# Moving the eight Toeplitz copies of a decoder layer's bias from ScalarE's queue to SyncE's

## The reference, cut to what matters

```
def step(S, xs):
    q_i, k_i, vw_i, kcd_i, qk_i, g_i = xs
    v_new = vw_i - jnp.einsum('bhck,bhkv->bhcv', kcd_i, S)
    o_i = ... + jnp.einsum('bhij,bhjv->bhiv', qk_i, v_new)
    S = S * jnp.exp(g_end)[..., None, None] + jnp.einsum('bhck,bhcv->bhkv', ..., v_new)
```

## Time and profile before

| what | us |
|---|---|
| median of 3 runs | 3125.3 (3123.02 to 3129.53) |
| the profiled execution, its own time | 3125.3 |
| its span, first to last instruction | 3123.6 |
| `delta_rule` in the profile, about | 775 to 1127 |

### The profile page before, as it was taken

How to read it: one execution, slowest core, us unless ns; L and a number is a source line. 1 busy time by engine, 2 the same in 40 slices (tenths; PEclk the granted TensorE clock), 3 DMA queues, 4 the chain that set the end, 5 groups by cost and what they waited for, 6 DMA issues and landing times. The chain is left out here.

```text
span 3123.6 us, 53938 instructions
## 1 busy us (share of the span) xinstructions
PE 2768.1 (89%) x22092; PEld 2499.9 (80%) x22092; DVE 1328.7 (43%) x2374; ACT 861.2 (28%) x1595; POOL 666.5 (21%) x499
## 2 busy tenths in 40 slices
PE   8999999998777859997559999877899999999996
PEld 7999999998566735554229999864699999999996
DVE  5999986130333456663123453031223332323224
ACT  4333112131222337772123122041222112121222
POOL 1222212111333200001224334100042122212223
PEclk9999999999788889996559999998699999999998
DMA  4112252322655430004654441214111111111111
GB/s 168 55 50 93 88 106 83 96 72 92 200 159 164 133 129 30 30 1 155 222 166 166 143 161 41 90 67 190 54 48 42 48 48 48 41 48 48 41 48 63
DMA packets 152232, 290.91 MB, mean 93 GB/s; under 512 B 29163, under 2 KB 97708, under 8 KB 149589
## 3 DMA queue, kind: packets, MB, share of 16 engines
q1 hardware_dynamic: 128278, 242.93, 24.1%
q0 software_dynamic: 9984, 27.28, 2.9%
q10 hardware_dynamic: 13728, 17.31, 1.6%
HBM read 246.50 MB, written 51.93 MB: 96 GB/s over the span
## 5 line engine op out<-in xcount | busy, mean ns | idle before, releaser
L152 POOL TENSOR_TENSOR mlp_w_low<-mlp_w_raw,mlp_w_high 128x1024 fp32r<-128x1024 f32 x72 | 173.7, 2412 | 853.5 <-ACT mlp_w_high L148 853.5
L336 PE MATMUL in_psum<-x_high,in_w_high 128*128 128x352 f32 x1416 | 266.8, 330 | 24.2 <-DVE x_low L531 14.3
L152 POOL TENSOR_TENSOR in_w_low<-in_w_raw,in_w_high 128x1024 fp32r<-128x1024 f32 x59 | 145.2, 2462 | 575.6 <-ACT in_w_high L148 575.6
L2728 PE MATMUL mlp_psum<-mlp_in,mlp_w_high 128*128 128x352 f32 x1536 | 264.9, 324 | 0.0
L336 PEld LDWEIGHTS in_psum<-x_high,in_w_high 128*128 128x128 f32 x1416 | 236.7, 191 | 32.8 <-issue 17.5
L336 PE MATMUL in_psum<-x_low,in_w_high 128*128 128x352 f32 x1416 | 259.8, 325 | 0.0
L336 PE MATMUL in_psum<-x_high,in_w_low 128*128 128x352 f32 x1416 | 258.6, 324 | 0.0
L2728 PEld LDWEIGHTS mlp_psum<-mlp_in,mlp_w_high 128*128 128x128 f32 x1536 | 251.2, 189 | 0.2
L148 ACT ACTIVATE mlp_w_high<-mlp_w_raw 128x1024 fp32r<-128x1024 f32 x72 | 76.4, 1061 | 622.1 <-PE mlp_psum L2728 617.8
L336 PEld LDWEIGHTS in_psum<-x_low,in_w_high 128*128 128x128 f32 x1416 | 235.8, 190 | 0.0
L336 PEld LDWEIGHTS in_psum<-x_high,in_w_low 128*128 128x128 f32 x1416 | 234.3, 189 | 0.0
(11 more groups left out here) (462 smaller groups left out, 4601.4 us busy)
## 6 DMA issues: line engine op xcount, KB each, us to landing
mlp_w_raw<-in_w_mlp SPq DMA_DIRECT2D x64, 512.0 KB, 3.4
in_w_raw<-in_w_in SPq DMA_DIRECT2D x59, 512.0 KB, 4.2
u_scratch<-stage SPq DMA_DIRECT2D x32, 528.0 KB, 5.2
gdnp_page_ring<-in_cache_cmp POOLq DMA_DIRECT2D x128, 128.0 KB, 3.4
gdnp_page_ring<-in_cache_cmp SPq DMA_DIRECT2D x128, 128.0 KB, 3.3
aux<-u_scratch SPq DMA_DIRECT2D x24, 528.0 KB, 4.1
ss_ring<-in_cache_slc SPq DMA_DIRECT2D x96, 128.0 KB, 3.9
ss_ring<-in_cache_slc ACTq DMA_DIRECT2D x80, 128.0 KB, 4.0
```

Source lines behind the costliest of these rows:

```text
L152: self.nc.gpsimd.tensor_tensor(self.low[:, i % 2, 0:k * P], self.raw[:, i % 2, 0:k * P], self.high[:, i % 2, 0:k * P].bitcast(F32), ALU.su ...
L336: return mm(psum[:, e % 2, n, 0:WN], w[:, i % 2, c * P:(c + 1) * P], a[:, c, n * WN:(n + 1) * WN], start=x == 0 and c == 0, stop=x == 2 an ...
L2728: return mm(psum[:, e % 2, n, 0:WN], w[:, i % 2, c * P:(c + 1) * P], a(c)[:, column(n)], start=x == 0 and c == 0, stop=x == 2 and c == CHU ...
```

## The change

The two DMAs of `spread_bias(i)` are no longer issued by ScalarE in rounds 0, 2, 4 and 6 but by SP in rounds 0, 1, 2 and 3. In SP's loop they stand after `load(t + 2)` and ahead of the page loads of the round. The copies themselves, their sizes, their access patterns and their semaphore are the same.

```diff
@@ delta_rule, block.sync
             for t in range(NT):
                 if t + 2 < NT:
                     load(t + 2)
+                if t < NSA_HEADS // 2:
+                    rows, toeplitz = spread
+                    for off, m, to in ((0, TP, 0), (LB_FULL, 640, TP)):
+                        src = bass.AP(rows.tensor, 2 * t * (LB_FULL + LB_WIN) + off + P - 1, [[LB_FULL + LB_WIN, 2], [-1, P], [1, m]])
+                        sp.dma_start(toeplitz[2 * t:2 * t + 2, :, to:to + m], src).then_inc(rows_spread, 16)
                 for step in range(t * STEPS + RING, min((t + 1) * STEPS + RING, NB * STEPS)):
                     load_pages(sp, step, (0, 1), pages_in)
                 if t + 1 < NT:
@@ delta_rule, block.scalar
-            def spread_bias(i):
-                rows, toeplitz = spread
-                for off, m, to in ((0, TP, 0), (LB_FULL, 640, TP)):
-                    src = bass.AP(rows.tensor, 2 * i * (LB_FULL + LB_WIN) + off + P - 1, [[LB_FULL + LB_WIN, 2], [-1, P], [1, m]])
-                    act.dma_start(toeplitz[2 * i:2 * i + 2, :, to:to + m], src).then_inc(rows_spread, 16)
-
@@
             for t in range(NT):
                 behind = t >= 1
-                if t % 2 == 0:
-                    spread_bias(t // 2)
                 row_decay(t + 1)
                 keep_y(t, 1)
```

## The result

The changed kernel takes 3160.8 us (median of 4 runs, 3158.7 to 3166.2) against 3124.2 us before: a ratio of 1.0117, 95% interval 1.0099 to 1.0137. The profiled execution took 3165.1 us, so its rows show 39.6 us more span where the medians differ by 37. Every time in this document is of executions in the faster of two states of the chip; one execution of the kernel with half of the rows, at 5840.7 us, is left out.

The account below looks back on a forecast made before the run. TensorE, busy 2768.1 of 3123.6 us, was taken as the bound. Copies ahead of SP's pages delay round 7 by 88.0 us, ScalarE's 29 us gain included: 3123.6 + 88.0 + 1.7 = 3213 us; range 3165 to 3255 us.

Parts of the forecast that it names:

- The rival in which pages pass the copies inside one queue: In SP's queue, pages are served while copies are pending; only ScalarE's 29 us are left, 3096 us; chance 0.12.
- I take 44: A pair of copies in SP's queue holds its two DMA engines for 44 us, bounds 37.8 to 51.
- lag: In SP's queue, the copies' rows begin to move 5 us after issue, bounds 3 and 7.
- landing: The first SP page behind a pair lands 2 us after the pair, at most 3.
- R: Moment of `compress(t, 4)` in a round, after its wait for SP's page; 848 us in round 0, then every 66.2 us.
- my lower end: For the pair, 37.8 us at 45 GB/s; for the whole main case, 58.0 us a round and 3178 to 3183 us.
- R to copies: SP issues the next round's first page DMAs, then gate and tile loads, before the next pair: 15.2 us.
- After round 7 nothing changes: Behind the start of round 7 in `delta_rule`, nobody waits for the copies any more: 0 us.
- Page landings of 30 us or more: Sign of being right: SP's pages behind a pair in rounds 0 to 3 land in 30 us or more.
- SP stalls on pages too: Rival: with SP's queue full, page issues wait for room, up to 8 us more a round, 3245 us; chance 0.08.
- 29 us for ScalarE: Idleness before `row_decay` in rounds 0, 2 and 4, beyond TensorE's 3.62 us, is freed: 29.0 us.
- the point of decision: Page waits may grow from 26.8 by 29 to 56 us, 14 for each of four pairs; above that the change loses.

Follow-up runs that it names:

- the kernel with half of the rows: Changed kernel, but each pair in rounds 0 to 3 copies 64 of 128 rows per head, the rest after SP's loop: 3100.7 us, ratio 0.9928.

## Why the prediction was right in direction and wrong in size

**Right: what decides.** That SP's pages would queue behind the copies on two engines, that the wait would sit at the fifth compress of rounds 0 to 3, that ScalarE's issue waits would go, and that nothing behind the block would change much. The dose of copies, the outer dimension and the change of queue each moved the time the way this theory says, and the increments of the page semaphores show the wait itself, on two engines of sixteen. The rival in which pages pass the copies inside one queue fell.

**Wrong: how long a pair holds the engines.** The step is "I take 44", with lag and landing 51 us from the issue of the copies to R. The trace has 850.21 to 891.05, 905.57 to 945.65 and 960.16 to 1000.25 us: 40.8, 40.1 and 40.1. Row by row it gives each term: in rounds 1 to 3 it was 3.8 to 4.5 us from issue to the first row where I took 5, 35.2 to 35.3 us of copies where I took 44 (36.1 in round 0), and 1.1 us from the last row to R where I took 2. The pair of before, from first row to last, took 47.3 to 49.4 us and not 51, which was the length of my window.

My reason for 44 was that POOL's pages go on sharing the two engines. They do, but only for half of the time (DMA queues of the changed kernel in 812:820 and, last, in 820:828; timeline of POOL):

```profile
q1 hardware_dynamic: 81, 0.33, 10.1%
q0 software_dynamic: 173, 0.45, 19.4%
...
q1 hardware_dynamic: 129, 0.41, 12.7%
```

```profile
815.64 0.54 POOL L714 DMA_DIRECT2D gdnp_page_ring<-in_cache_cmp  x1 [0.61 <-issue]
841.13 0.58 POOL L714 DMA_DIRECT2D gdnp_page_ring<-in_cache_cmp  x1 [23.40 <-issue]
```

Beside POOL's pages the copies ran at 41 GB/s, and without them at 51. POOL issues no page between 816.2 and 841.1 us: its next page needs a place in the ring, and TensorE, which frees it, stands waiting for SP's page. The wait that the copies make also clears the engines for them. And the 45 GB/s of before, in a stretch in which hardly anything else moved, was not the most that the two engines do; why it was lower there is open. SP's own pages and tile loads, which shared the engines before, now stand behind or ahead of the pair; how much of the 47 to 49 us was theirs and how much POOL's, no run here separates. I had nearly the right number as my lower end, 37.8.

Summed up to the start of round 7, where I forecast 88.0 us, and the trace has 42.4 (43.1 less 0.65 by which the block began later):

| step | forecast | measured | us |
|---|---|---|---|
| R of round 0, less the 0.65 | 848 | 838.2 | -9.8 |
| three times copies to R | 153.0 | 121.0 | -32.0 |
| three times R to copies | 45.6 | 40.4 | -5.2 |
| R to `row_decay` of round 4 | 13.9 | 13.2 | -0.7 |
| rounds 4 to 6 | 83.1 | 85.2 | +2.1 |

The first two lines are 42 of the 46 us: the pair itself is 34 of them, and lag, landing and start make the other 8. "R to copies" was 11.4 in round 0 and 14.5 in the others, where I had taken 15.2 from a round whose pages came in one by one; after a pair they land together. The lower granted clock after the wait was there as expected. The window view of the changed kernel, right behind the first wait (columns as in rows 8):

```profile
838.00:850.00 12.00, 11.08 (x164) 8.41 (x164) 4.95 (x17) 3.27 (x12) 4.33 (x8) 0.50 0.57 162
```

The range failed mostly by the same step. My lower end kept 42.8 us from copies to R (3 + 37.8 + 2) where the trace has 40.1 to 40.8, and 15.2 from R to the copies where it has 14.5: 58.0 us a round, and the trace has 54.6. With the round 0 that makes +53 us up to round 7 where the trace has +42. A smaller step failed beside it: "After round 7 nothing changes" put at nothing what was 3.5 us. The profiled execution, 3165.1 us, is as slow as the low end of the range; the median is 4 us below it.

**Wrong: three of the signs.** Rounds of 60 to 75 us (they took 53.4 to 54.6) and a `delta_rule` 55 to 125 us longer (42) are the same step. Page landings of 30 us or more were the wrong thing to look for. The longest in the view is 19.9 us, for the page whose issue began at 811.2, and that is 831.1: the view takes the sixteenth increment of a semaphore, but two pages share this one, and 28 of their 32 were there by 831.5. The two pages were complete only at 838.76, 27.6 us after that issue began. That is still under 30, since SP's hold of 13 us had put the issue itself off.

The rival "SP stalls on pages too" came half true: one page issue in each of the four rounds took 16.1 to 16.9 us. It cost nothing extra, because in round 0 it ended at 827.7, and the copies moved until 837.74.

**Wrong in the rivals: 29 us for ScalarE.** The forecast did not use it as a term, but the faster rival did, and put the point of decision at 14 us of page waits a pair. Taking away the hold, with one copy a round, brought 10 us. An idle stretch in front of an engine is not its price when the next thing that it leads to is late as well.

## What to carry to other kernels

Before moving a DMA to another queue, ask what stands behind it there, and how many engines it uses: a pair of copies with an outer dimension of 2 kept two engines for 35 to 36 us, and every load behind it in the queue needed those two. What helped most was shape and place together: one pair over all eight heads, issued where nothing but stores followed, took 1.9% off the kernel before; with another shape alone, still on SP's queue ahead of the pages (outer dimension 8, or 16 groups of columns), the time was 1.2 to 1.3% below it. And a duration measured while two streams share an engine is no estimate for either alone; the row of a stretch in which it ran alone was the better one. Before letting a stream go on sharing in an estimate, ask whether it can go on at all while the rest waits.

## What the runs showed of the hardware that was not expected

- The hold of the issuing queue depends on what is already in it. Two copies of 128 rows on each of two engines held SP or ScalarE for some 12 to 14 us, and over eight heads, again 128 rows an engine and copy, for 11 to 16 us. One such copy was issued in 0.6 to 2.4 us, and two of 64 rows in 1.4 to 3.7 us together, but the first page behind them was then held for some 7 us. In the kernel before, the fourth pair was held for only 1.96 us, though it had the same shape; why is open.
- The engines of a copy followed the outer dimension at 2 and 8: 11.4% of sixteen and 47 GB/s at 2, 57.8% (with pages) and 212 GB/s at 8. The Trainium skill gives this rule in "DMA: Bandwidth & Descriptors", section "Why a DMA increments its semaphore by 16 and not by 1", and the runs agree; they also agree with its section "Queues, rings and completion order", that a queue's descriptors are consumed in order on each engine: the last increments of SP's pages came 0.5 to 1.0 us behind the last row of the copies in rounds 1 to 3.
- Streams in different queues share an engine, and each is slowed. The copies ran at 51 GB/s alone and at 41 beside POOL's pages (820:828 and 812:820). Beside SP's own loads and POOL's, in three queues, a pair took 47 to 49 us instead of 35 to 36, with landings of up to 16.9 us in the view.
- A landing in the view is the sixteenth increment of a semaphore. Where two loads share a semaphore it can come before either is complete: 831.1 us for two pages that were complete at 838.76.
